# Attention: softmax's reciprocal sums spread through DRAM by GpSimd, and two banks for the value products

## What is computed

```python
s = jnp.einsum('bqkgd,btkd->bkgqt', q, k).astype(jnp.float32) * (HEAD_DIM ** -0.5)
p = jax.nn.softmax(s, axis=-1).astype(v.dtype)
return jnp.einsum('bkgqt,btkd->bqkgd', p, v)
```

## Time and profile before

| | |
|---|---|
| three runs, us | 2625.05, 2626.34, 2624.3 |
| span of the profiled execution, us | 2625.6 |
| TensorE matmul busy | 98% |
| TensorE weight load busy | 73% |
| VectorE busy | 51% |
| ScalarE busy | 32% |
| GpSimd busy | 33% |

### The profile page before, as it was taken

The page is one execution under the profiler, slowest core; times in us unless marked ns, Lnnn a source line. Parts: engine busy times, 40 slices in busy tenths (PEclk is TensorE's granted clock), DMA queues, the critical chain, the costliest instruction groups (busy, mean ns, idle before and its releaser), DMA issues.

```text
span 2625.6 us, 40326 instructions
## 1 busy us (share of the span) xinstructions
PE 2575.6 (98%) x15424; PEld 1910.1 (73%) x15424; DVE 1327.4 (51%) x2373; ACT 829.9 (32%) x1783; POOL 856.6 (33%) x716
## 2 busy tenths in 40 slices
PE   5899999999999999999999999999999999999999
PEld 2677777775788878888884567765555567778887
DVE  3455555551555567777842256533224513753324
ACT  3334444442312122222002347731111223663221
POOL 0222222220555525556543222022323043103444
PEclk9999999999999999999999999999999999999999
DMA  6211111113145434454322210001111122101222
GB/s 222 70 45 46 38 45 45 33 33 145 65 145 184 153 114 159 167 185 161 134 89 70 88 50 24 1 33 65 57 56 57 56 85 81 41 1 49 97 81 96
DMA packets 61410, 220.93 MB, mean 84 GB/s; under 512 B 6784, under 2 KB 8960, under 8 KB 60992
## 3 DMA queue, kind: packets, MB, share of 16 engines
q1 hardware_dynamic: 42576, 153.11, 17.2%
q0 software_dynamic: 14656, 56.89, 6.3%
q10 hardware_dynamic: 4016, 8.65, 0.9%
HBM read 214.90 MB, written 2.15 MB: 83 GB/s over the span
## 4 chain that ended last, share of the span: by engine, by line
PE 94%; DVE 2%; DMA 1%; ACT 1%; issue 1%; ACTq 0%; POOL 0%; DVEq 0%; SPq 0%
PE psum L456 90%; PE psum L969 3%; DMA arena<-in_conds 1%; DMA arena<-in_stream 1%; PE psum L1027 0%; ACTq L1284 0%; PE psum L689 0%; ACT arena L1423 0%; DVE arena L2047 0%; DVE arena L2019 0%; ACT arena L1393 0%; PE psum L652 0%; ACT arena L1411 0%; POOL arena L2743 0%; DVE arena L2080 0%
## 5 line engine op out<-in xcount | busy, mean ns | idle before, releaser
L456 PE MATMUL psum<-arena 128*128 128x256 f32 (+10 forms) x14544 | 2473.0, 352 | 46.2 <-DVE arena L1765 12.5
L456 PEld LDWEIGHTS psum<-arena 128*128 128x128 f32 (+4 forms) x14544 | 1815.6, 170 | 685.8 <-issue 252.8
L2789 POOL TENSOR_TENSOR arena<-arena 128x512 f32<-128x512 f32 (+1 forms) x104 | 137.6, 1323 | 772.5 <-DMA arena<-in_stream 399.5
L2034 DVE TENSOR_TENSOR arena<-psum,arena 128x256 f32<-128x256 f32 (+1 forms) x103 | 47.3, 459 | 291.2 <-PE psum L456 282.1
L2005 DVE SCALAR_TENSOR_TENSOR arena<-arena 128x1024 f32<-128x1024 f32 x128 | 170.8, 1383 | 0.0
L2040 DVE TENSOR_TENSOR arena<-psum,arena 128x256 f32<-128x256 f32 (+1 forms) x103 | 47.5, 461 | 234.1 <-PE psum L456 230.1
L2793 POOL TENSOR_TENSOR arena<-arena 128x512 f32<-128x512 f32 (+1 forms) x104 | 133.2, 1280 | 96.0 <-PE psum L456 90.5
L2800 POOL TENSOR_TENSOR arena<-arena 128x512 f32<-128x512 f32 (+1 forms) x104 | 144.3, 1388 | 36.9 <-PE psum L456 36.6
L2797 POOL TENSOR_TENSOR arena<-arena 128x512 f32<-128x512 f32 (+1 forms) x104 | 138.1, 1328 | 45.2 <-PE psum L456 38.5
L1447 ACT ACTIVATE arena<-psum 128x256 f32<-128x256 f32 (+1 forms) x103 | 42.7, 414 | 307.1 <-PE psum L456 307.1
L2743 POOL TENSOR_TENSOR arena<-arena 128x512 f32<-128x512 f32 x16 | 22.1, 1402 | 315.1 <-ACT arena L1356 315.1
(11 more groups left out here) (281 smaller groups left out, 1826.9 us busy)
## 6 DMA issues: line engine op xcount, KB each, us to landing
arena<-in_stream SPq DMA_DIRECT2D x288, 512.0 KB, 3.8
arena<-in_mods POOLq DMA_DIRECT2D x80, 512.0 KB, 5.8
arena<-gc_rows POOLq DMA_DIRECT2D x16, 384.0 KB, 4.8
arena<-in_bias POOLq DMA_DIRECT2D x16, 384.0 KB, 3.9
arena<-in_xT ACTq DMA_DIRECT2D x2, 1024.0 KB, 14.0
arena<-in_conds ACTq DMA_DIRECT2D x1, 1536.0 KB
arena<-arena POOLq DMA_DIRECT2D x4, 384.0 KB, 4.3
out<-arena SPq DMA_DIRECT2D x3, 512.0 KB, 6.1
```

The lines of the kernel that those rows point to most:

```text
L456: return pe.matmul(out, lhsT, rhs, start=start, stop=stop, skip_group_check=True)
L2789: add(sums[0], a21, a22, ALU.add).then_inc(s("wsum"), 1)
```

## The change

- `widen` (ACT), `spread` (PE), `copy_sums` (ACT) and the buffer `inv_sums` go.
- `recip` writes to a new buffer `recs`, one half for each of two groups in turn.
- POOL gets `write_sums(u)`: when a unit's reciprocals are there, it writes them to the DRAM tensor `sum_rows`, with the queries along a row. That is 128 x 2 single float32 elements in one transfer, and two such transfers for a context unit.
- POOL gets `spread_sums(u)` at the end of a group: it waits until the group's writes have landed, and then issues two transfers that read a row of `sum_rows` each and broadcast it to 64 partitions. Their targets `rsums` are `sqb[:, 1]` and `rnorm` in turn.
- The value products of group n go to bank 6 + n % 2, and `values` waits only for the `to_att` of the group before the last.
- `to_att` comes one round later (`u - 4`) and waits for the transfers (`sums_in`).
- ACT no longer waits for the last `to_att` before the z stage.
- In POOL's list `write_sums(u)` and `spread_sums(u)` stand behind the table loads and negations of unit `u`. The first of the four z weight sums moves to the place behind unit `near + 4`, and the others stay behind all units.

```diff
--- before.py
+++ after.py
@@ -124,6 +124,7 @@
         arena = ctx.enter_context(nc.sbuf_tensor("arena", [P, 53000], F32))
         psum = ctx.enter_context(nc.psum_tensor("psum", [P, 8, 512], F32))
         gc_rows = nc.dram_tensor("gc_rows", (2 * HEADS, TOK), F32).ap()
+        sum_rows = nc.dram_tensor("sum_rows", (3 * 2 * PAIRS, 2, SEQ), F32).ap()
         sems = {}
 
         def s(name):
@@ -288,7 +289,8 @@
         rsum_at = sp2.at - SEQ
         HT2 = sp2.take(4 * 4 * WIDE)
         snaps2 = sp2.take(WIDE), sp2.take(WIDE), arena[:, rsum_at:rsum_at + WIDE]
-        inv_sums = arena[:, rsum_at + SEQ + 16 * WIDE:][:, 0:4 * P].rearrange("p (a b) -> p a b", a=2)
+        recs = sp2.take(2, 2 * XC)
+        rsums = sqb[:, 1, 0:SEQ], rnorm[:, 0:SEQ]
         MG2 = arena[:, MG2_AT:MG2_AT + KT * TOK].rearrange("p (a b) -> p a b", a=KT)
         n2 = Region(MG2_AT, 53000)
         hsq, hrn, rt1 = n2.take(2, TOK), n2.take(2, TOK), rsum
@@ -366,6 +368,12 @@
         def att_before(l, p):
 
             return 2 * p if l == 0 else 4 * PAIRS + p
+
+        def blocks_before(group):
+
+            both = 2 * PAIRS
+            return (XC + CC) * (group // 2) + XC * (group % 2) if group <= 2 * both else \
+                (XC + CC) * both + XC * (group - 2 * both)
 
         def biased(p, q):
 
@@ -984,10 +992,13 @@
                     near = biased(p, q)
                     pe.wait_ge(s("at_ptc"), g + u + 1)
                     pe.wait_ge(s("at_ptx"), tx_before(l, u + 1))
+                    if u == 0:
+                        pe.wait_ge(s("b2_vb"), 2 * l + 2)
                     if u == len(us) - 1:
                         first_z()
-                    if b == 0 and (g + u):
-                        pe.wait_ge(s("at_att"), att_before(l, p) + q)
+                    group = att_before(l, p) + q
+                    if b == 0 and group >= 2:
+                        pe.wait_ge(s("at_att"), group - 1)
                     if near and b in (1, 2):
                         pe.wait_ge(s("at_vs"), 32 * (l + 1))
 
@@ -1010,23 +1021,10 @@
                         for c in chunks:
                             for a in range(2):
                                 at = prob_at(a, c, b2)
-                                m = mm(psum[half(a), 6, (b + b2) * P:(b + b2 + 1) * P], weight(a, c),
+                                m = mm(psum[half(a), 6 + group % 2, (b + b2) * P:(b + b2 + 1) * P], weight(a, c),
                                        PT[:, u % 2, at:at + P], c == chunks[0], c == CH - 1)
                                 if c == CH - 1 and (not q or b2):
                                     m.then_inc(s("at_pv"), 1)
-
-                def spread(u):
-
-                    p, q, b = us[u]
-                    pe.wait_ge(s("at_wide"), g + u + 1)
-                    if u == 0:
-                        pe.wait_ge(s("b2_vb"), 2 * l + 2)
-                    if b == 0 and (g + u):
-                        pe.wait_ge(s("at_rc"), att_before(l, p) + q)
-                    for b2 in range(CC if q else 1):
-                        m = pe.transpose(psum[:, 7, (b + b2) * P:(b + b2 + 1) * P],
-                                         inv_sums[:, u % 2, b2 * P:(b2 + 1) * P], ident)
-                    m.then_inc(s("at_rs"), 1)
 
                 for u in range(len(us) + 2):
                     if u < len(us):
@@ -1036,7 +1034,6 @@
                     if 1 <= u <= len(us):
                         transposes(u - 1)
                     if u >= 2:
-                        spread(u - 2)
                         values(u - 2)
 
             for l in range(2):
@@ -1576,34 +1573,13 @@
                                   bias=st[:, 0, o:o + 1], accum_out=st[:, 1, o:o + 1])
                         m.then_inc(s("at_P"), 1)
 
-                def copy_sums(u):
-                    p, q, b = us[u]
-                    act.wait_ge(s("at_rs"), g + u + 1)
-                    act.wait_ge(s("at_att"), att_before(l, p) + q)
-                    w = CTX if q else SEQ
-                    f(rsum[:, 0:w], psum[:, 7, 0:w], ACT.Copy).then_inc(s("at_rc"), 1)
-
-                def widen(u):
-                    o, n = stat(u, 0), CC if us[u][1] else 1
-                    act.wait_ge(s("at_ri"), g + u + 1)
-                    if g + u >= 2:
-                        act.wait_ge(s("at_rs"), g + u - 1)
-                    for b2 in range(n):
-                        v = st[:, 2, o + b2:o + b2 + n + 1:n, None].to_broadcast([P, 2, HD])
-                        m = f(inv_sums[:, u % 2, b2 * P:(b2 + 1) * P].rearrange("p (a d) -> p a d", a=2), v, ACT.Copy)
-                    m.then_inc(s("at_wide"), 1)
-
-                for u in range(len(us) + 3):
-                    if 1 <= u <= len(us):
+                for u in range(len(us) + 1):
+                    if u:
                         evict(u - 1)
-                    if 2 <= u < len(us) + 2 and last(us[u - 2]):
-                        copy_sums(u - 2)
                     if u < len(us):
                         exps(u)
                     if u == 0:
                         context_values()
-                    if 1 <= u <= len(us):
-                        widen(u - 1)
 
             for l in range(2):
                 wide = l == 0
@@ -1657,7 +1633,6 @@
                         .then_inc(s("b2_vb"), 1)
 
                 attention(l, context_values)
-                act.wait_ge(s("at_att"), att_before(l, 2 * PAIRS))
                 w = half_of(l)
                 banks = (0, 2, 3), (1, 2, 3)
                 ended = None
@@ -2430,21 +2405,26 @@
                     dve.tensor_copy(PT[:, u % 2, SEQ:2 * SEQ], score_banks(l, u)[:, SEQ:2 * SEQ]).then_inc(s("at_ptc"), 1)
 
                 def recip(u):
-                    o, n = stat(u, 0), 4 if us[u][1] else 2
+                    p, q, b = us[u]
+                    o, n = stat(u, 0), 2 * CC if q else 2
+                    group = att_before(l, p) + q
                     dve.wait_ge(s("at_P"), 2 * (g + u) + 2)
-                    dve.reciprocal(st[:, 2, o:o + n], st[:, 1, o:o + n]).then_inc(s("at_ri"), 1)
+                    if b == 0 and group >= 2:
+                        dve.wait_ge(s("sums_out"), 16 * blocks_before(group - 1))
+                    dve.reciprocal(recs[:, group % 2, 2 * b:2 * b + n], st[:, 1, o:o + n]).then_inc(s("at_ri"), 1)
 
                 def to_att(u):
                     p, q, b = us[u]
-                    dve.wait_ge(s("at_rc"), att_before(l, p) + q + 1)
+                    group = att_before(l, p) + q
+                    dve.wait_ge(s("sums_in"), 32 * (group + 1))
                     dve.wait_ge(s("at_pv"), 2 * (g + u + 1))
                     w, at = (CTX, SEQ) if q else (SEQ, 0)
-                    stt(ATT[:, p, at:at + w], psum[:, 6, 0:w], 0.5, rsum[:, 0:w], ALU.mult, ALU.mult)\
-                        .then_inc(s("at_att"), 1)
-
-                for u in range(len(us) + 3):
-                    if u >= 3 and last(us[u - 3]):
-                        to_att(u - 3)
+                    stt(ATT[:, p, at:at + w], psum[:, 6 + group % 2, 0:w], 0.5, rsums[group % 2][:, 0:w], ALU.mult,
+                        ALU.mult).then_inc(s("at_att"), 1)
+
+                for u in range(len(us) + 4):
+                    if u >= 4 and last(us[u - 4]):
+                        to_att(u - 4)
                     if u < len(us):
                         maxima(u)
                     if u == 0:
@@ -2881,6 +2861,34 @@
                     qk_sums(n)
                 negate_tables(0)
                 negate_tables(1)
+                def write_sums(u):
+
+                    p, q, b = us[u]
+                    n = att_before(l, p) + q
+                    pool.wait_ge(s("at_ri"), g + u + 1)
+                    for b2 in range(CC if q else 1):
+                        at = (b + b2) * P
+                        pool.dma_start(sum_rows[n, :, at:at + P].rearrange("a p -> p a"),
+                                       recs[:, n % 2, b2:2 * CC:CC] if q else recs[:, n % 2, 2 * b:2 * b + 2],
+                                       allow_slow_non_contiguous=True).then_inc(s("sums_out"), 16)
+
+                def spread_sums(u):
+
+                    p, q, _ = us[u]
+                    n, w = att_before(l, p) + q, CTX if q else SEQ
+                    pool.wait_ge(s("sums_out"), 16 * blocks_before(n + 1))
+                    if n >= 2:
+                        pool.wait_ge(s("at_att"), n - 1)
+                    for a in range(2):
+                        pool.dma_start(rsums[n % 2][half(a), 0:w],
+                                       sum_rows[n, a:a + 1, 0:w].to_broadcast([HD, w])).then_inc(s("sums_in"), 16)
+
+                def z_sums(j):
+
+                    t = T0 + L_Z + 2 * j
+                    weight_sums(pair_at(l, N_Z) + j, weights(pool, t), weights(pool, t + 1), 4, WS2)
+
+                near = max(u for u in range(len(us)) if us[u][0] < PAIRS)
                 for u in range(len(us)):
                     p, q, b = us[u]
```

(13 more changed lines are left out.)

## The result

2749.03 us, median of 5 runs (2746.82 to 2754.36), against 2625.7 (2624.3 to 2630.01) of the kernel before on the same chip: ratio 1.0466, 95% interval 1.0454 to 1.0478. The change costs 4.7%; I had forecast 2623.2. The profiled run took 2754.36 us, its span is 2752.6.

A forecast was written before the change was run, and what follows sets the result against it. The prediction took TensorE, busy in 98% of the span, as the bound. Removed transposes -9.0, late tables in layer 1 +3.7 and layer 0 stalls +3.4 gave -1.9: span 2623.7, runs' median 2623.2 us, range 2616 to 2633.

The forecast's parts named there:

- I take 2.5 us for landing: GpSimd's write of a unit's reciprocals to DRAM: assumed to land 2.5 us after issue.
- +5 us per microsecond: Both attention layers: each microsecond of later landing adds +2 us in layer 1 and about +3 in layer 0.
- alone, a group is hidden, by 1.35 us: Near groups: the reciprocals' round trip alone fits the allowance with 1.35 us spare; far ones have 4 us or more.
- 5.95 in my sum and 7.3 allowed: From a group's last `recip` until `to_att` can run: 5.95 us predicted, 7.3 us allowed in near units.
- POOL needs 17.6 us for a pair ... that is the whole mechanism: Layer 0, pairs with a table: GpSimd's list takes 17.6 us where TensorE needs 15.6; stalls together +3.4 us.
- The slot of 0.117 us: TensorE's transposes in attention: each of 80 removed reciprocal transposes saves 0.117 us, -9.4 us in all.
- the rival of 0.2 us: TensorE's transposes: the gap behind each goes too, so 15.3 us are saved instead of 9.4; 2617.3 us, chance 0.10.
- Layer 1's late tables: Layer 1: two bias tables load behind the previous pair's spreading and stall about 2 us each, +3.7 us.
- The second bank "counts nothing": Value products in attention: a second bank gains 0, since no `values` waits for its `at_att` in the earlier trace.
- The slower one: Rival on GpSimd's writes: single elements land late; at 4.5 us landing, +8 and 2633 us; chance 0.24.
- The reciprocals do not pay: Rival on TensorE: removed transposes were hidden behind ScalarE, about +7 us; counted within the slower case's chance of 0.24.
- Hides better: Rival on the round trip: 2.0 us landing and 2.8 for spreading shorten stalls, -5.6, 2619.4 us; chance 0.19.

The follow-up runs named there:

- e2: The changed kernel without the reciprocals' writes and all waits for them; spreading transfers read constants: 2625.23 us, ratio 0.9988 to the kernel before.
- e10: The changed kernel with single elements written 16 B apart in DRAM, spreading transfers reading constants, waits kept: 2633.62 us, ratio 1.0023 to the kernel before.
- e6: The changed kernel with each query's two reciprocals written as one 8 B run, so sums reach other columns: 2648.9 us, ratio 1.0085 to the kernel before.
- e1: The kernel before plus seven small probe transfers on GpSimd's queue and one on SyncE's, each GpSimd one waited for: 2634.08 us against 2628.51.
- e7: The kernel before plus seven probe writes of single elements to DRAM, at varied distance and number: 2629.36 us against 2627.33.
- e5: As e4, but writes issued from ScalarE's queue behind the next unit's exponentials, with three semaphores: 2620.63 us, ratio 0.9974 to the kernel before.
- e3: The changed kernel with VectorE turning reciprocals first, so GpSimd writes 128 B runs in 160 transfers: 2635.79 us, ratio 1.0035 to the kernel before.
- e4: As e3, with bias tables loaded one unit earlier, ahead of writes and spreading, and negated two units earlier: 2634.05 us, ratio 1.0019 to the kernel before.
- e8: As e5, with value products in bank 6 alone and a wait for the last `to_att`: 2681.29 us, ratio 1.0214 to the kernel before.

## Why the prediction was wrong, step by step

| landing of a write | kernel | time against before |
|---|---|---|
| none | e2 | -3.3 us |
| 2.1 us | e10 | +6.7 us |
| 3.4 us | e6 | +21.6 us |
| 8.0 to 9.5 us | the change | +123.3 us |

In e2 and e10 the spreading pairs read constants in place of the sums.

**"I take 2.5 us for landing"**: this term failed. It is 8.0 alone (e1) and 8.0 to 9.5 in the chain above. I took it from the `gc_rows` row, sixteen runs of 3 KB, and argued from bytes and idle queues. e1 and e7 show that elements side by side were the point. The Trainium skill (DMA: Bandwidth & Descriptors, Anatomy of one DMA) gives about 2.0 us plus bytes for a transfer from GpSimd. The runs of 128 and 512 B and the elements 16 B or more apart land a little below it (1.5 to 1.8 us); elements side by side, with 8.0, do not follow it. I had said that no row speaks for or against one descriptor per element; given that, the upper end of 6.8 belonged in the range, and I let it end at 4.5.

**"+5 us per microsecond"**: this slope failed too, and would have done so with the right landing: at 8.5 us, about the mean of the landings in that chain, it gives -1.9 + 6 x 5 = +28, measured +123. It counted two late tables and a lag of GpSimd's list. But "alone, a group is hidden, by 1.35 us" means that beyond 2.5 + 1.35 = 3.85 us each near group stalls by itself, and I said that far ones have 4 us or more, which 8.5 uses up as well. From 2.1 to 3.4 us the table has a slope of 11, from 3.4 to 8.5 one of 20 us per microsecond. Between e6 and the change TensorE's waits in the attention layers grow from 18.4 to 100.0 us, 16 per microsecond of landing, and its busy time from 2575.7 to 2602.8 us, 5 per microsecond. The chain was 13.5 us, against 5.95 in my sum and 7.3 allowed: 0.29 until the issue (I had 0.06), 9.46 for landing (2.5), 0.29 for waking (0.28) and 3.45 for the spreading pair (3.1). TensorE's first stall is 5.61, about the difference of 6.2.

**The lower clock** was not in the sum: 37.8 us (e5 above). A stall of several us is paid again in the matmuls behind it.

**"POOL needs 17.6 us for a pair ... that is the whole mechanism"**: the mechanism is right and the size is not. It is 18.15 us with landing at 2.1 (e10) and 31.8 in the change. e10 is +6.7 where my own sum at 2.1 us gives -1.9 - 0.4 x 5 = -3.9. Of these 10 us 6.4 are TensorE's busy time over that of e5; the longer list (table pair 5.25, not 4.5; issue of a write 0.72, not 0.55) is seen, but I have no run that prices it. e3 to e5 confirm the mechanism from the other side. With turned writes, which land after 1.6 us from GpSimd's queue (the profile gives no landing on ScalarE's), taking them off the list gives 12.2 us (e4 at +5.5, e5 at -6.7 against before); the order of the tables by itself gives 1.7, less than e3 and e4 can tell.

**The slot of 0.117 us** is right: the near period fell from 3.23 to 3.12 (e2, e5), far ones from 4.87 to 4.76, and the gap of 0.17 stayed (before the weights at 1575.93 in e5), which ends the rival of 0.2 us. **Layer 1's late tables** are in the right place and too small. At a landing of 2.1 us my sum gives stalls of 1.6 and 1.3 us; in e10 TensorE stands 3.09 and 1.49. In e2, with no write and no landing before the loads, the sum leaves none (negation done at 2272.4 - 2.8 = 2269.6, need at 2270.4), and TensorE still stands 2.10 and 1.07. There GpSimd issues layer 1's first pair 2.6 us after its reciprocal (2257.70), with no releaser shown, and sees the second table 7.0 us after its issue (2272.15 to 2279.15), not 4.5 to 5.0. **The second bank "counts nothing"** is right only of the old order; with the later `to_att` it is worth 61 us (e8).

**The rivals.** The slower one named the mechanism and the place, with 0.24 for it, and undersized both of its factors. "The reciprocals do not pay" falls: e5 is faster by 0.26%. "Hides better" took 2.0 us of landing and gave -5.6: e10, at 2.1, is +6.7, and even e2, without landing, gains only 3.3.

## What to carry to other kernels

A transfer of single elements into DRAM costs by how they lie there: turn them on chip first and write runs of 128 B, or probe the landing alone before the step is built around it. A round trip through DRAM should not be waited for in a list in which other transfers stand behind the wait: with the tables earlier in the list and the writes on ScalarE's queue (e5), 6.7 of the 9.0 us of gain were left. When a delay passes its margin, price it by the number of places at which it is paid, and add the clock.

## What the runs showed of the hardware

- Landing, GpSimd's queue: 256 single float32 side by side in two DRAM rows 8.0 us, 128 in one row 7.2, 64 6.8, 32 3.3, 16 1.6; 128 at 8 B distance 3.5, at 16 B 1.7, 32 B 1.7, 64 B 1.8, 512 B 1.7; 128 runs of 8 B side by side 3.1; 8 runs of 128 B 1.5; 256 single elements into SBUF 2.4. Why the distance matters stays open.
- SyncE's queue isn't faster at it: 10.0 us for the 256 elements (e1).
- The issue of such a write holds GpSimd for 0.73 us, that of 8 runs of 128 B for 0.50.
- After waits of 5.61 (the change) and 2.33 us (e8) TensorE's next 24 matmuls took 3.99 and 3.43 us instead of 2.17, at a mean granted clock of 0.50 and 0.59; after one of 1.82 (e8) they took 2.17.
